# Three unused tiles shift the tiles that TensorE streams to multiples of 1024 bytes

## What is computed

```
first_block:   mod = silu(c) @ w_ada + b_ada                        # six vectors
               h = modulate(rmsnorm(x)); proj = h @ w_in            # 1024 -> 11264
               o_sb = stick_breaking_attention(16 heads of 64)
               o_ret = silu(r_g) * head_rmsnorm(retention(4 heads)) # 256 -> 512
               x += gate1 * ((g_sb * o_sb @ w_proj_sb + g_ret * o_ret @ w_proj_ret) @ w_out)
               x += gate2 * (silu(a) * u) @ w_ffn_out               # a, u = h @ w_ffn_in, 1024 -> 2 x 2816
second_block:  proj = rmsnorm(x) @ w_in_2                           # 1024 -> 3384
               attention over the 128 best keys of an index score, and gated linear attention
               x += concat(o_a, o_b) @ w_out_2
               x += (silu(h @ w_ffn_gate) * (h @ w_ffn_up)) @ w_ffn_down
return rmsnorm(x)
```

## Time and profile before

| | |
|---|---|
| median of 3 runs | 1862.66 us (1862.33 to 1863.74) |
| span of the profiled execution | 1861.7 us; no other time of this execution is listed |
| TensorE busy | 1802.7 us, 97% |
| VectorE, ScalarE, GpSimd busy | 975.9, 804.4, 800.2 us |
| mean granted TensorE clock | 0.991 |

### The profile page before, as it was taken

One profiled execution on the slowest core, in us unless ns is written; L12 is line 12 of the kernel. 1 busy time (PEld: TensorE's weight loads), 2 busy tenths in 40 slices (PEclk: granted clock), 3 DMA queues, 4 the chain that ended last, 5 costly groups with the idle time before them and its releaser, 6 DMA issues.

```text
span 1861.7 us, 25246 instructions
## 1 busy us (share of the span) xinstructions
PE 1802.7 (97%) x9884; PEld 1466.5 (79%) x9884; DVE 975.9 (52%) x1602; ACT 804.4 (43%) x1358; POOL 800.2 (43%) x607
## 2 busy tenths in 40 slices
PE   6999999999999999998999999999999999999997
PEld 4677778878778777886998899777776679988985
DVE  6666561424251303327663465648777667635754
ACT  4555552224232323335552354535546555424542
POOL 4634344636365544431540253044556227504730
PEclk9999999999999999998999999999999999999999
DMA  7421122544433222322433233432221113342332
GB/s 281 155 68 60 55 68 91 200 151 152 145 125 122 68 90 68 136 90 72 124 102 116 78 102 102 115 96 80 91 91 58 50 49 108 97 130 69 105 94 74
DMA packets 158871, 192.11 MB, mean 103 GB/s; under 512 B 10345, under 2 KB 141689, under 8 KB 158370
## 3 DMA queue, kind: packets, MB, share of 16 engines
q1 hardware_dynamic: 156898, 181.77, 30.0%
q0 software_dynamic: 1104, 5.24, 1.0%
q10 hardware_dynamic: 752, 3.49, 0.5%
HBM read 188.37 MB, written 4.72 MB: 104 GB/s over the span
## 4 chain that ended last, share of the span: by engine, by line
PE 87%; DVE 8%; ACT 3%; issue 1%; DMA 0%; POOL 0%; DVEq 0%; SPq 0%; ACTq 0%
PE bank L1756 19%; PE bank L1761 19%; PE bank L1758 19%; PE bank L1788 7%; PE bank L1790 6%; PE bank L1786 6%; PE bank L1865 2%; PE bank L1799 2%; DVE stg L2077 1%; PE bank L1815 1%; DVE wl L2270 1%; PE bank L1835 1%; PE bank L1851 1%; DVE left L2107 1%; PE bank L2014 1%
## 5 line engine op out<-in xcount | busy, mean ns | idle before, releaser
L1756 PE MATMUL bank<-hH,wh 128*128 128x512 f32 x1072 | 443.6, 414 | 8.5 <-ACT tmps L2813 5.4
L1758 PE MATMUL bank<-hH,wl 128*128 128x512 f32 x1072 | 424.9, 396 | 0.0
L1761 PE MATMUL bank<-hL,wh 128*128 128x512 f32 x1072 | 424.9, 396 | 0.0
L2968 POOL TENSOR_TENSOR wl<-stg,wh 128x512 fp32r<-128x512 f32 x150 | 202.7, 1351 | 488.7 <-ACT wh L2573 488.4
L2573 ACT ACTIVATE wh<-stg 128x1024 fp32r<-128x1024 f32 (+2 forms) x222 | 216.7, 978 | 223.3 <-PE bank L1761 189.3
L1756 PEld LDWEIGHTS bank<-hH,wh 128*128 128x128 f32 x1072 | 202.5, 189 | 72.1 <-issue 23.3
L3023 POOL TENSOR_TENSOR wl<-stg,wh 128x512 fp32r<-128x512 f32 x120 | 166.0, 1392 | 199.7 <-ACT wh L2766 199.5
L1761 PEld LDWEIGHTS bank<-hL,wh 128*128 128x128 f32 x1072 | 202.2, 189 | 49.3 <-DVE hL L2223 0.3
L1758 PEld LDWEIGHTS bank<-hH,wl 128*128 128x128 f32 x1072 | 202.7, 189 | 44.1 <-issue 2.6
L2969 POOL TENSOR_TENSOR wl<-stg,wh 128x512 fp32r<-128x512 f32 x150 | 204.5, 1363 | 0.0
L2077 DVE CUSTOM_DVE_ANT_0 stg<-stg,cb,col 128x1024 f32<-128x1024 f32 x48 | 82.4, 1750 | 83.3 <-DMA stg<-in_w_ada_t 83.3
(11 more groups left out here) (361 smaller groups left out, 3925.3 us busy)
## 6 DMA issues: line engine op xcount, KB each, us to landing
stg<-in_w_in SPq DMA_DIRECT2D x54, 1024.0 KB, 5.2
stg<-in_w_ada_t SPq DMA_DIRECT2D x48, 512.0 KB, 4.6
stg<-in_w_ffn_in SPq DMA_DIRECT2D x22, 1024.0 KB, 5.1
stg<-in_w_ffn_gate SPq DMA_DIRECT2D x11, 1024.0 KB, 5.3
stg<-in_w_ffn_up SPq DMA_DIRECT2D x11, 1024.0 KB, 5.3
stg<-in_w_proj_ret SPq DMA_DIRECT2D x8, 1024.0 KB, 5.1
stg<-in_w_out SPq DMA_DIRECT2D x8, 1024.0 KB, 5.1
stg<-in_w_ffn_out SPq DMA_DIRECT2D x8, 768.0 KB, 4.8
```

The source lines that it names most:

```text
L1756: T.matmul(ps, wh, xh, start=j["first"] and k == 0, stop=False)
L1758: T.matmul(ps, wl, xh, start=False, stop=False)
L1761: t = T.matmul(ps, wh, xl, start=False, stop=j["stop"] and last)
L2968: G.tensor_tensor(lo[:, 0:h, :], src[:, 0:h, :], hi[:, 0:h, :], ALU.subtract)
```

## The change

Three calls of `sb` are added whose tiles no instruction reads or writes. They take 448, 992 and 896 bytes per partition.

```diff
@@ -1345,6 +1345,7 @@
         small = sb("small", [P, 320])
+        sb("to_kilobyte", [P, 112])
         XR = sb("XR", [P, KT, S])
@@ -1404,6 +1405,7 @@
             brow = sb("brow", [P, 640], ctx=ph)
+            sb("to_kilobyte_a", [P, 248], ctx=ph)
             TH, TL, HF, TF = {}, {}, {}, {}
@@ -1433,6 +1435,7 @@
             tmp9 = sb("tmp9", [P, S], ctx=ph)
+            sb("to_kilobyte_2", [P, 224], ctx=ph)
             with ExitStack() as ph1:
                 GQ = sb("GQ", [P, 2, S], ctx=ph1)
```

## The result

The changed kernel takes 1864.83 us (median of 21 runs, 1864.16 to 1866.18) against 1861.69 for the kernel before (21 runs on the same chip, 1860.79 to 1863.74): ratio 1.0017, interval 1.0011 to 1.0023. That is 3.1 us slower, where I gave 2.6 us faster, and 4.7 above the 1860.1 that I gave; 1.0 of the 4.7 lies in the base, for which the first three runs had given 1862.66. The profiled executions show less of it: spans of 1862.8 and 1861.7 us at granted clocks of 0.992 and 0.991. In every run whose time and span are both listed, the time is 1.8 to 1.9 us above the span. So the traced execution of the kernel before was one of about 1863.5 us (an estimate from that distance), 1.8 above the median, and its start times are late by about as much.

The account below looks back on a forecast made before the run. The prediction took TensorE's own matmul rate to bound the kernel. Its sum was the span of 1861.7, minus 2.6 for the first feed-forward, plus 0.96 from span to median: 1860.1 us, range 1802 to 1870.

Parts of the forecast that it names:

- Only TensorE's own rate matters: Most of the span: nothing but TensorE's rate counts; it is busy for 1802.7 of 1861.7 us.
- the cost of the edit itself is nothing on every queue: All queues: the unused tiles add no instruction, wait or transfer, so the edit itself costs nothing.
- 0 us is the value I take: 4,992 matmuls of 512 columns: offsets 576, 608, 704 share one price, so no change; bounds 49.9 us less, 22.0 more.
- should mostly run short: First feed-forward, 1,680 matmuls of 256 columns: 4.4 ns less each, 7.4 us at most, 2.6 taken; chance 0.31.
- The sign that I had named: First feed-forward: tLa's median bar falls from 280 to 276 ns if offset modulo 64 kept it long.
- I take 0 for it: Second feed-forward, 256 columns: mixed in its first half, short in its second, so a change of 0 us.
- The 35% that passes: Pairs of groups in the feed-forwards: 0.26 of 0.74 us arrives past the wait at DVE, making 7.4 us 2.6.
- Streamed tile and weights fall on the same place: Rival, all float32r matmuls: both starting at 0 modulo 128 costs 4.4 ns a matmul; 1887 us, chance 0.22.
- Nothing moves: Rival, whole kernel: the phase in which a run starts sets spacing, not the tile; 1862.7 us, chance 0.18.
- Crossings: Rival, float32r matmuls: each multiple of 1024 crossed costs 10.0 ns at 512 columns; 60.4 us less, 1802 us, chance 0.27.

Follow-up runs that it names:

- experiment 2: Changed kernel with the weight tiles wh and wl (and tmps, ident, small tiles) 64 bytes further, streamed tiles still at 0 modulo 1024; 1847.02 us, ratio 0.9918.
- experiment 4: Two kernels: the changed one with all streamed tiles at 128 modulo 1024 (first, 1848.75 us), then at 896 (1849.50 us); weights unmoved.
- experiment 1: Kernel before with the 992-byte tile alone: tHa, tLa, fHa, fLa go from 608 to 576 modulo 1024; 1856.95 us, ratio 0.9970.
- experiment 5: Changed kernel with all streamed tiles at 704, 768 or 832 modulo 1024, weights unmoved; 1847.53, 1865.01 and 1857.28 us.
- Experiment 6: Changed kernel with only the second feed-forward's streamed tiles moved, to 64 modulo 1024 (distance 192, as before); 1859.69 us, ratio 0.9988.
- experiment 3: Changed kernel with streamed tiles at 576 and weights at 192 and 704 modulo 1024, keeping the changed kernel's distance; 1864.72 us, ratio 1.0012.
- experiment 7: Changed kernel with streamed tiles at 128 and wl (with tmps) 64 bytes further: distance 0 to wh, 192 to wl; 1857.73 us, ratio 0.9978.
- Experiment 9: Changed kernel with 512-column tiles at 128 (distance 0) and tHa, tLa, h2H, h2L, tHb, tLb at 320 (distance 192); 1837.62 us, ratio 0.9872.

## Why the prediction was wrong

**"Only TensorE's own rate matters" and "the cost of the edit itself is nothing on every queue": right in the main.** The line durations of DVE and the half-rate passes did not move, and TensorE's spacings alone give the sign in every row of the table and most of the size; its waits take up a part.

**512 columns, "0 us is the value I take": wrong in size, and in its reason.** It was -0.93 x 4,992 = -4.6 us. The reason was that three offsets show one price. They don't bear it out: 576 and 608 are the distances 192 and 224, both slow (233.3 and 233.2 ns between starts), and goH at 704 is distance 64, but its matmuls come with waits between them, so that only 36 of them have a free neighbour (232.6 ns). The bars of the earlier trace rows could not show what that distance does to an undisturbed stream. Experiments 2 and 4 show what was to be had: 3.9 and 5.5 ns, not the 10.0 of a crossing.

**The first feed-forward "should mostly run short" with every offset 0 modulo 64: the step that failed.** I took the likeness to the second feed-forward to be the offset modulo 64. It was the distance to the weights: 192 runs short, from 576 and from 832 (experiments 1 and 5), while 0 and 768, also multiples of 64, run long. It went from 117.6 to 118.7 ns, +1.8 us by the sum and +0.9 between the start times, where I had -2.6. That tHa at 608 keeps it long was right: experiment 1, in which it is the 256-column tile that changes its distance, gains 5.4 us. The sign that I had named came true: tLa's median bar did not fall (280 to 281 ns). Before, the spacing was 118.4 ns behind tHa, 116.8 behind hH, which runs between them at distance 192, and 114.3 behind h2H.

**The second feed-forward, "I take 0 for it": the largest miss.** It was mostly short (mean 114.3) and went to 118.8: +7.5 us by the sum, 5.0 by the start times. That is more than the whole 3.1 us of the result. Experiment 6 gives 5.1 of it back by 64 bytes. I moved tiles that ran at the short spacing from 576 to 0 and priced only the hope of the others to become short; the rule "0 modulo 64" covered both offsets, so I didn't see the risk. The rows themselves, where the good state stands at one offset only, did not support the rule that widely.

**The 35% that passes: wrong, and it isn't one number.** Experiment 1 passes 0.57 of 0.56 us a pair, and 4.9 of 5.6 over the first feed-forward (its last use of tLa comes 7.0 us earlier than before, its first 2.1). Where the spacing grows less passes: 5.0 of 7.5 in the second feed-forward of the changed kernel, 3.7 of 7.3 at distance 0, while TensorE's waits get shorter. The two stretches of the earlier trace rows differ in more than their spacing, so their difference is no measure of pass-through; the 1.70 us on DVE in the earlier trace rows is part of both. Had the first step been right, it would have paid 5.4, not 2.6.

**The rivals.** "Streamed tile and weights fall on the same place" named the right kind of relation and the right sign, at 0.22. Its place was wrong: modulo 128 both 128 and 0 are the same place, and 0 is the best for 512 columns. So was its price: the 4.4 ns arose in the 256-column matmuls of the second feed-forward alone, and the 512-column ones got faster. "Nothing moves" was closest of the four cases to the time, 2.1 us off (3.1 with the base of 21 runs), and by luck: -4.6 cancels part of +9.3 in the sum. "Crossings" is refuted by experiments 2 and 3. The argument that I held against the same-place case, that the weights alternate between 128 and 640 and the spacing takes no notice, only says that the period divides 512.

The page of the Trainium skill that I weighed, "SBUF — State Buffer", section "Who interferes with whom", has TensorE's two read ports independent. By it experiment 2 would do nothing; moving the weight tiles by 64 bytes took 17.8 us off, so here the measurement decides against it.

## What to carry to other kernels

When TensorE is bound by full-rate float32r matmuls, try the address of the streamed tile relative to the weight tile, modulo 256, for each matmul width by itself: here distance 0 was best for 512 columns and 192 for 256, worth 1.3% together, for six unused strips of SBUF. Don't infer a rule of alignment from tiles that share one weight address, and measure the distance between starts, not the bars. When an edit moves a thing that already is in the good state, price its loss as well as the gain of the rest.

## What the runs showed of the hardware that I had not expected

The distance between starts of float32r matmuls, with nothing else changed, ran from 227.7 to 233.3 ns at 512 columns and from 113.9 to 119.9 at 256, set by the distance from weights to streamed tile modulo 256 in steps that aren't smooth (512 columns: 0, 32, 64, 128, 192 bytes give 227.7, 233.2, 229.3, 232.4, 233.3). The order of the distances is another for the two widths: 0 is the best for one and the worst for the other. What inside the chip makes it so stays open; that the reads of the two tiles meet in SBUF is argued from experiment 2, not shown. The weight loads do change as well: the bars of those beside 256-column matmuls last 188 ns in the changed kernel and 192 in the first kernel of experiment 4, where narrow is longest:

```profile
L1789 PEld LDWEIGHTS bank<-tHa,wh 128*128 128x128 f32 x320 | 60.2, 188 | 0.3
```

```profile
L1789 PEld LDWEIGHTS bank<-tHa,wh 128*128 128x128 f32 x320 | 61.3, 192 | 0.3
```

Also open are the distances 96, 160 and most odd multiples of 32, and why one weight tile's distance raises its neighbours' spacing too (experiment 7).

Experiment 9's time gained 5.2 us less than its spacings. In its second block 3.5 us of 6.4 arrive, while TensorE's idle time there grows from 7.9 to 9.4 us. Ahead of the first feed-forward 15.8 arrive by tLa's first use (863.1 against 878.9), or 13.7 without the 2.1 by which the trace of before is late, where the spacings give 16.4; where these 2.7 went stays open. The page of the profile agrees in that DVE holds more of the path there than in the changed kernel (its line of shares by engine, experiment 9, then changed):

```profile
PE 85%; DVE 9%; ACT 3%; issue 2%; DMA 0%; DVEq 0%; POOL 0%; SPq 0%; ACTq 0%
```

```profile
PE 88%; DVE 7%; ACT 3%; issue 1%; DMA 0%; POOL 0%; DVEq 0%; SPq 0%; ACTq 0%
```
